# Gate and up products of a gathered expert in four strips of 128 columns, gate before up, and one turn of the hidden values

## The chip, the cores and the metric

One core of a Trainium2 chip runs one program. The time is the device time of one execution in microseconds (us); the program before was timed three times, and the median counts.

## The reference, cut to what matters

Two blocks on 256 tokens of 1024 values. The first holds two layers of four kinds of attention; the second a modulated layer with differential attention and pooling, and then a mixture of 32 experts in four groups. All is float32. The change lies in the experts:

```python
g_logits = (xt @ w_rg) + b_rg                 # 4 groups, the best one is taken
e_logits = ((xt @ w_re) + b_re).reshape(N, 4, 8)
top_p, top_i = lax.top_k(softmax(e_logits[tok, g_sel]), 2)
weights = g_p[:, None] * top_p / sum(top_p)
# for each expert e, over the tokens that chose it:
#   hidden = silu(x @ w_gate[e]) * (x @ w_up[e])      1024 -> 512
#   y     += weight * (hidden @ w_down[e])            512 -> 1024
x = x + g2 * y
```

Each expert has three matrices of 2 MiB: gate and up of 1024x512, down of 512x1024.

## The kernel before, in words

**Stages.** The attention layers and the projections come first, with weights loaded through a ring of six places of 2 MiB in SBUF (`ring`). The expert stage begins on TensorE after the router. Where no expert has more than 32 tokens (`crowd` is 0), it takes the gathered way, which this run takes; the dense way beside it is not executed.

**The gathered way.** Experts go in eight quads of four (`four_experts`, q the quad, s the expert in it). `gather` picks the tokens of a quad by a product with a selection matrix into `XG`, 32 columns for each expert. For an expert, TensorE does this:

- `gate_up` (lines 2400 to 2432): x times gate and x times up, in bank 1 of PSUM. The stationary side is the expert's 32 columns of `XG` for one of eight blocks of the contraction (k), so a product fills 32 of the array's 128 columns, and four strips stand side by side. Strips 0 and 1 are gate, 2 and 3 up; each holds half of the 512 hidden columns, 256 of them, namely columns 4f + 2(j mod 2) and the one behind it, two of every four. For each k all four strips follow each other. The last expert does its gate strips first and its up strips then. One increment of `g_gu` marks the end.
- ScalarE takes silu of gate on 64 partitions x 256 (line 943, `SIG`), VectorE multiplies by up (line 1737, `HID`).
- `turn_hidden` (lines 2434 to 2445) turns `HID` by two products with the identity, each reading every second column; ScalarE copies the result (line 950, `HG`).
- `down` (lines 2447 to 2463): four blocks of the hidden values, four strips of 256 output columns each; VectorE scales and stores them (line 1746), and `add_outputs` (line 2478) adds a quad's outputs to the sums.

Between these, quads interleave: after the first expert of a quad come `add_outputs` of the quad before and `turn_spread` (line 2470), after the second and third the two halves of the next `gather` (line 2398), and none of these after the fourth.

**The order of the loads.** All loads are issued by SP in an order written out by hand (lines 458 to 567). Experts 0 to 3 are loaded into the ring and into dead buffers before the stage. After the router's flag, `load_gathered` (line 529) waits for the place's last reader and issues one load: gate and up places are free with `g_gu`, down places with `g_down`. The order is gate, up and down of expert 4, then down of 3, gate and up of 5, gate of 6, down of 5, and from expert 6 on in turn; gate of every third expert of a quad lies in `probs` and waits for the one four before. A waiting load holds back all loads behind it. Down of expert 31 comes in two halves.

Of the kernel before, what the change touches and what calls it, by code (L numbers as in the profile page):

```python
# [8 lines left out]
P = 128  # L9
# [3 lines left out]
KD = D // P  # L13
# [6 lines left out]
NE = 32  # L20
FC = 4
CAP = 32
# [65 lines left out]
def build(nc, x, ab_w, ab_out_w, cd_w, cmp_w1, cmp_w2, uq_w, ukv_w, cd_out_w, ada_w, ada_b, in_w, pool_mt, pool_w,  # L88
          router_w, out_w, norm_rows, gate_w, up_w, down_w, consts, smalls, out):
    F32, BF16, U8 = mybir.dt.float32, mybir.dt.bfloat16, mybir.dt.uint8  # L90
    ALU, ACT, AX = mybir.AluOpType, mybir.ActivationFunctionType, mybir.AxisListType
    ctx = ExitStack()
    with ctx:
# [10 lines left out]
        def stages(suffix, adds):  # L104
            at = 0
            for tag, n in adds:
                stage_of[tag + suffix], before_stage[tag + suffix] = "all" + suffix, at
                at += n
# [5 lines left out]
        stages("_Ta", [(s[0], s[2]) for s in turned_stages])  # L114
        stages("_Tv", [(s[0], s[3]) for s in turned_stages])
        stages("_mm", [("abin", 12), ("about", 4), ("cdin", 12), ("cdout", 4), ("win", 8), ("wout", 4)])
        stages("_Pa", [("abin", 6), ("cdin", 6), ("win", 4)])
        stages("_Pv", [("abin", 6), ("cdin", 6), ("win", 4)])

        def upto(name, n):  # L120

            return sem(name), before_stage.get(name, 0) + n

        def sem(name):
            name = stage_of.get(name, name)
            if name not in made:
                made[name] = ctx.enter_context(nc.semaphore("s_" + name))
            return made[name]
# [38 lines left out]
        bank = [banks[:, i, :] for i in range(8)]  # L167
# [9 lines left out]
        def const(name, rows=P):  # L177
            a, n = CO[name]
            return C[0:rows, a:a + n]
# [5 lines left out]
        ident = const("ident")  # L185
# [38 lines left out]
        qt_flat = QT[:, :, :].rearrange("p a n -> p (a n)")  # L224
# [2 lines left out]
            return qt_flat[:, a:a + n].rearrange("p (k n) -> p k n", k=k)  # L227

        XG = part(0, 1024, KD)
        SIG = qt_flat[64:128, 2048:2304]  # L230
        HID = qt_flat[0:64, 2304:2560]
        HG = qt_flat[:, 2560:2688]
        ones = qt_flat[:, 2688:2816]
        YE = qt_flat[:, 2816:3840]
# [122 lines left out]
        def first_quad(q):  # L357
            return isinstance(q, int) and q == 0
# [8 lines left out]
        def hidden_psum(q):  # L367

            return bank[3] if last_quad(q) else bank[2][:, 256:512]
# [16 lines left out]
        def gathered_landed(eng, q, s, j):  # L386

            slot = eslot(3 * (s % 2) + j)
            if (s, j) == (2, 0):
                eng.wait_ge(*upto("ahead0", q * 16 + 16))  # L390
                return
            if not first_quad(q):
                if (s, j) == (0, 0):
                    eng.wait_ge(*upto(f"slot{slot}", q * 16 + (loads_of[slot] + 16)))
                    return
                skipped = 0 if s % 2 == 1 and j == 2 else 1
                eng.wait_ge(*upto(f"slot{slot}", q * 32 + (loads_of[slot] + 16 * (s // 2 + 1 - skipped))))
                return
            e = s
            ahead = {(2, 1): ("ahead1", 64), (2, 2): ("ahead2", 48), (3, 0): ("ahead3", 32),  # L400
                     (3, 1): ("ahead4", 16 * len(up3_homes))}
            if (e, j) in ahead:
                eng.wait_ge(*upto(*ahead[e, j]))
                return
            eng.wait_ge(*upto(f"slot{slot}", loads_of[slot] + 16 * (e // 2 + 1)))
# [15 lines left out]
        def _(sp):  # L421
# [7 lines left out]
            off, n, k, src = first_rows  # L429
            sp.dma_start(ring[0][:, off:off + n].rearrange("p (k n) -> p k n", k=k), src).then_inc(sem("ld_first"), 16)  # L430
            for i, (name, parts, _) in enumerate(chunks):
# [4 lines left out]
                if i >= SLOTS:  # L436
                    s, n = chunks[i - SLOTS][2]
# [90 lines left out]

            def load_gathered(j, e, freed_by):

                sp.wait_ge(*upto("g_down" if j % 3 == 2 else "g_gu", freed_by + 1))
                if e % 4 == 2 and j % 3 == 0:
                    load_third_gate(e)
                else:
                    load_expert(j, e)
# [69 lines left out]
        def _(act):  # L605
# [130 lines left out]
            act.activation(QT[:, 12, :], bank[5][:, 0:256], ACT.Copy).then_inc(sem("abi_Ta"), 1)  # L736
            query_squares(2, 1, scrA[:, 1536:2048])
            for t in range(NT):
                act.wait_ge(*upto("idx", t + 1))
                for odd in range(2):  # L740
                    act.activation(index_relu(t, odd), index_psum(t, odd), ACT.Relu).then_inc(sem("idx_r"), 1)
            act.wait_ge(*upto("ms", ROOT["abk1"]))
# [196 lines left out]
            def gathered_silu(e):  # L939
                act.wait_ge(*upto("g_gu", e + 1))  # L940
                if e > 0:
                    act.wait_ge(*upto("g_hid", e))
                act.activation(SIG, bank[1][0:64, 0:256], ACT.Silu).then_inc(sem("g_sig"), 1)  # L943

            def take_hidden(e):

# [28 lines left out]
        def _(v):  # L975
# [403 lines left out]
            pe = small("pe")  # L1379
# [6 lines left out]
            for half in range(2):  # L1386
                for g in range(2):
                    n = 16 - half
# [36 lines left out]
            a = SM["kvlat_col"][0]  # L1425
# [3 lines left out]
            a = SM["qlat_col"][0]  # L1429
# [111 lines left out]
            a = SM["lambdas"][0]  # L1541
# [191 lines left out]
            def hidden(e):  # L1733
                v.wait_ge(*upto("g_sig", e + 1))
                if e > 0:
                    v.wait_ge(*upto("g_ht", e))
                v.tensor_tensor(HID, SIG, bank[1][64:128, 0:256], ALU.mult).then_inc(sem("g_hid"), 1)  # L1737

            def outputs(e):

# [26 lines left out]
            with v.If(crowded == 0):  # L1767
                for e in range(NE):
                    q = e // 4
# [37 lines left out]
        def _(pe):  # L1807
# [240 lines left out]
            for t in range(NT):  # L2048
                K = P * (t + 1)
                for h in range(4):  # L2050
                    r = slice(64 * (h % 2), 64 * (h % 2) + 64)
                    ins = pe.matmul(bank[(2, 6)[t] + h % 2][:, (h // 2) * SEQ:(h // 2) * SEQ + K],
                                    QT[r, 10 + h // 2, t * P:(t + 1) * P], QT[r, 12, 0:K], start=True, stop=True)
                ins.then_inc(sem("idx"), 1)
            for t in range(NT):
                project_ab(3, t)
            pe.wait_ge(*upto("ab_k", 2))
# [82 lines left out]
            for g in range(2):  # L2140
                pe.matmul(bank[6][0:N_CMP, 64 + 64 * g:128 + 64 * g], hcT[:, 16 * g:16 * g + N_CMP], lat[:, 2560:2624],
                          start=True, stop=True)
# [259 lines left out]
            def gate_up(q, s):  # L2402

                e, last = expert_of(q, s)
                if s == 0:
                    pe.wait_ge(*upto("g_xc", q * 2 + 1))
                if not (first_quad(q) and s == 0):
                    pe.wait_ge(*upto("g_hid", e))
                wg, wu = gathered_weight(q, s, 0), gathered_weight(q, s, 1)

                def strip(k, j):
                    wk = (wg, wu)[j // 2](k).rearrange("p (f c) -> p f c", c=FC)
                    return pe.matmul(bank[1][CAP * j:CAP * j + CAP, 0:256], XG[:, k, CAP * s:CAP * s + CAP],  # L2413
                                     wk[:, :, 2 * (j % 2):2 * (j % 2) + 2], start=(k == 0), stop=(k == KD - 1))

                gathered_landed(pe, q, s, 0)
                if last:
                    for k in range(KD):
                        for j in range(2):
                            strip(k, j)  # L2420
                    gathered_landed(pe, q, s, 1)
                    for k in range(KD):
                        for j in range(2, 4):
                            ins = strip(k, j)
                else:
                    gathered_landed(pe, q, s, 1)
                    for k in range(KD):
                        if first_quad(q) and s == 0 and k == 4:
                            pe.wait_ge(*upto("g_xv", 1))
                        for j in range(4):  # L2430
                            ins = strip(k, j)
                ins.then_inc(sem("g_gu"), 1)

            def turn_hidden(q, s):

                e, last = expert_of(q, s)
                pe.wait_ge(*upto("g_hid", e + 1))
                if last_quad(q):
                    pe.wait_ge(*upto("g_hc", e))
                elif not (first_quad(q) and s == 0):  # L2440
                    pe.wait_ge(*upto("g_ye", e))
                for j in range(2):
                    ins = pe.matmul(hidden_psum(q)[:, 64 * j:64 * j + 64], HID[:, j:256:2], ident[0:64, 0:64],
                                    start=True, stop=True)
                ins.then_inc(sem("g_ht"), 1)

            def down(q, s):

                e, last = expert_of(q, s)
                if not last:  # L2450
                    gathered_landed(pe, q, s, 2)
                pe.wait_ge(*upto("g_hc", e + 1))
                if last_quad(q):
                    pe.wait_ge(*upto("g_ye", e))
                wd = gathered_weight(q, s, 2)
                for c in range(FC):
                    if last and c % 2 == 0:
                        pe.wait_ge(*upto(f"last_down{c // 2}", 16))
                    a = 64 * (c % 2) + CAP * (c // 2)
                    for n in range(4):  # L2460
                        ins = pe.matmul(bank[2][CAP * n:CAP * n + CAP, 0:256], HG[:, a:a + CAP],  # L2461
                                        wd(c)[:, 256 * n:256 * n + 256], start=(c == 0), stop=(c == FC - 1))
                ins.then_inc(sem("g_down"), 1)

# [183 lines left out]
```

## Time and profile before

| | us |
|---|---|
| median of 3 executions | 910.43 |
| lowest, highest | 907.78, 912.58 |
| the profiled execution | 911.11 |
| its span | 909.3 |
| TensorE busy in the span | 775.5 (85%) |
| VectorE, ScalarE busy | 373.5, 168.4 |
| bytes moved, mean rate | 284.38 MB, 313 GB/s |

The profile is of one execution. Its span is shorter than that execution's time by 1.8 us, which lie around it. Busy time of TensorE counts pipelined products, so a busy TensorE isn't at its peak. The granted clock of TensorE is given as a share of 2.4 GHz; it has two levels, 1.2 and 2.4 GHz, and a value between them is a mean over a stretch.

### The profile page before, as it was taken

Reading aid. Unit: us, or ns where it says so; the run is one execution under the profiler, and the core shown is the slowest. Engines: PE = TensorE matmul, PEld = TensorE weight load, DVE = VectorE, ACT = ScalarE, POOL = GpSimd, SP = SyncE. Lnnn points to the kernel's source line nnn. Section 1 sums busy time; section 2 is a strip of 40 time slices with the busy share of each in tenths; the row PEclk is TensorE's granted clock in tenths of the full one; section 3 lists DMA queues with packets and bytes.
Section 4 is the critical chain, followed back from the end, with each engine's and each line's share of the span. In section 5 each row is a group of like instructions: output and inputs, shape, how many; then the busy total and the mean of one; then the engine's idle time right before and its main releaser. Section 6 shows DMA issues by size and latency. Waiting matters only on the chain.

```text
span 909.3 us, 13058 instructions
## 1 busy us (share of the span) xinstructions
PE 775.5 (85%) x5393; PEld 465.6 (51%) x5393; DVE 373.5 (41%) x885; ACT 168.4 (19%) x473; POOL 40.5 (4%) x36
## 2 busy tenths in 40 slices
PE   7999899999998999999999987858766686677655
PEld 3544664456476644456578573535534444344332
DVE  2478668557854676766441212111111111121113
ACT  3222630223356301041120100000010100001001
POOL 1110000012400000001000000000000000000000
PEclk9999999999999999999999997889899889899888
DMA  9984506765002749987679999999999999999994
GB/s 343 394 291 155 186 1 241 269 231 186 1 1 82 277 130 352 392 338 321 232 269 396 406 425 430 430 430 427 426 427 429 430 428 429 427 428 429 427 428 162
DMA packets 54555, 284.38 MB, mean 313 GB/s; under 512 B 2800, under 2 KB 7280, under 8 KB 41968
## 3 DMA queue, kind: packets, MB, share of 16 engines
q1 hardware_dynamic: 54512, 283.81, 78.0%
q8 instruction: 27, 0.44, 0.2%
q14 instruction: 16, 0.13, 0.0%
HBM read 282.75 MB, written 1.05 MB: 312 GB/s over the span
## 4 chain that ended last, share of the span: by engine, by line
PE 55%; DMA 34%; DVE 5%; issue 2%; ACT 2%; POOL 1%; SPq 1%; DVEq 0%; POOLq 0%
DMA ring<-in_up_w 30%; PE banks L2002 15%; PE banks L1850 9%; PE banks L2413 8%; PE banks L2248 4%; DMA ring<-in_down_w 3%; PE banks L1954 3%; PE banks L2461 2%; PE banks L1882 2%; PE banks L2398 2%; DMA ring<-in_ada_w 1%; PE banks L1929 1%; POOL rs L590 1%; PE banks L1980 1%; PE banks L2492 1%
## 5 line engine op out<-in xcount | busy, mean ns | idle before, releaser
L2413 PE MATMUL banks<-ring,QT 128*32 128x256 f32 x1696 | 143.0, 445 | 56.7 <-DMA ring<-in_up_w 56.7
L2002 PE MATMUL banks<-ring,hT 128*128 128x512 f32 (+4 forms) x384 | 157.9, 566 | 2.4 <-DMA ring<-in_ab_w 2.1
L2413 PEld LDWEIGHTS banks<-ring,QT 128*32 128x32 f32 x1696 | 71.9, 123 | 105.7 <-DMA ring<-in_up_w 44.1
L2002 PEld LDWEIGHTS banks<-ring,hT 128*128 128x128 f32 x384 | 72.4, 193 | 75.5 <-issue 68.6
L1746 DVE TENSOR_TENSOR QT<-banks,MOD 32x256 f32<-32x256 f32 x128 | 53.8, 421 | 138.5 <-PE banks L2461 137.2
L1737 DVE TENSOR_TENSOR QT<-QT,banks 64x256 f32<-64x256 f32 x32 | 13.5, 423 | 191.4 <-ACT QT L943 191.4
L1850 PE MATMUL banks<-ring,hT 128*128 128x512 f32 x192 | 83.9, 594 | 1.9 <-ACT hT L628 1.8
L2461 PE MATMUL banks<-ring,QT 128*32 128x256 f32 x992 | 66.0, 408 | 14.6 <-ACT QT L950 12.4
L590 POOL TENSOR_TENSOR rs<-st,mhalf 128x1 f32<-128x1 f32 (+7 forms) x27 | 33.3, 1237 | 863.3 <-DVE st L1783 451.7
L943 ACT ACTIVATE QT<-banks 64x256 f32<-64x256 f32 x32 | 12.0, 375 | 294.4 <-PE banks L2413 294.4
L1185 DVE SCALAR_TENSOR_TENSOR extra<-ring,cs,extra 128x512 f32<-128x512 f32 x84 | 63.1, 752 | 2.9
L2413 PE MATMUL banks<-probs,QT 128*32 128x256 f32 x256 | 41.6, 492 | 25.1 <-DMA ring<-in_up_w 25.1
L1850 PEld LDWEIGHTS banks<-ring,hT 128*128 128x128 f32 x192 | 36.0, 190 | 46.9 <-issue 43.1
L2398 PEld LDWEIGHTS banks<-Y 128*128 128x128 f32 x224 | 54.4, 334 | 6.1 <-issue 6.1
L2398 PE MATMUL banks<-Y 128*128 128x128 f32 x224 | 57.1, 408 | 0.0
L2248 PE MATMUL banks<-ring,hT 128*128 128x512 f32 x128 | 56.5, 596 | 0.2 <-DVE MOD L1193 0.2
L2461 PEld LDWEIGHTS banks<-ring,QT 128*32 128x32 f32 x992 | 37.1, 114 | 31.2 <-issue 18.7
L664 ACT ACTIVATE probs<-banks,soft 128x256 f32<-128x256 f32 (+1 forms) x96 | 39.9, 432 | 32.9 <-DVE soft L1104 31.1
L2413 PEld LDWEIGHTS banks<-probs,QT 128*32 128x32 f32 x256 | 21.0, 136 | 42.6 <-issue 38.9
L2248 PEld LDWEIGHTS banks<-ring,hT 128*128 128x128 f32 x128 | 23.8, 190 | 30.9 <-issue 28.4
L2478 PE MATMUL banks<-QT,Y 128*128 128x512 f32 x64 | 31.2, 632 | 1.9 <-DVE QT L1746 1.9
L1094 DVE TENSOR_REDUCE soft<-banks 128x4 f32<-128x1024 f32 (+1 forms) x24 | 24.0, 1002 | 16.7 <-PE banks L1893 15.1
(361 smaller groups left out, 767.6 us busy)
## 6 DMA issues: line engine op xcount, KB each, us to landing
ring<-in_down_w SPq DMA_DIRECT2D x30, 2048.0 KB, 21.8
ring<-in_up_w SPq DMA_DIRECT2D x30, 2048.0 KB, 23.6
ring<-in_gate_w SPq DMA_DIRECT2D x23, 2048.0 KB, 20.4
ring<-in_ada_w SPq DMA_DIRECT2D x12, 2048.0 KB, 15.4
probs<-in_gate_w SPq DMA_DIRECT2D x8, 2048.0 KB, 29.2
ring<-in_ab_w SPq DMA_DIRECT2D x4, 2048.0 KB, 19.4
ring<-in_cd_w SPq DMA_DIRECT2D x4, 2048.0 KB, 13.5
ring<-in_in_w SPq DMA_DIRECT2D x4, 2048.0 KB, 14.5
```

Source lines behind the costliest of these rows:

```text
L590: pool.tensor_tensor(rs[0:r, a:a + k], st2[0:r, a:a + k], mhalf[0:r, a:a + k], ALU.pow)\
L664: act.activation(PB[:, u % 2, h * K:(h + 1) * K], score_of(u, h), ACT.Exp, bias=nmx[:, 4 * u + h:4 * u + h + 1], scale=scale, accum_out=sm ...
L1185: ins = v.scalar_tensor_tensor(out=acc, in0=w[:, k, :], scalar=by, in1=acc, op0=ALU.mult, op1=ALU.add)
L1746: ins = v.tensor_tensor(YE[CAP * s:CAP * s + CAP, 256 * c:256 * c + 256], bank[2][CAP * c:CAP * c + CAP, 0:256], MOD[CAP * s:CAP * s + CAP ...
L1850: ins = pe.matmul(bank[j % 4][:, 0:n], hT[:, k, t * P:(t + 1) * P], w[:, k, :], start=(k == 0), stop=(k == KD - 1))
L1954: ins = pe.matmul(value_bank(u)[:, P * h:P * h + v.shape[1]], PTB[:, u % 2, kb, h * P:(h + 1) * P], v, start=(kb == 0), stop=(kb == nb - 1))
L2002: ins = pe.matmul(bank[b][:, 0:n], hT[:, k, t * P:(t + 1) * P], w[:, k, :], start=(k == 0), stop=(k == KD - 1))
L2248: ins = pe.matmul(win_bank(c, t)[:, :], hT[:, k, t * P:(t + 1) * P], w[:, k, :], start=(k == 0), stop=(k == KD - 1))
L2398: ins = pe.matmul(bank[3 * half][:, P * k:P * k + P], Y[:, t, 4 * half + k:D:KD], SEL[:, t, :], start=(t == 0), stop=(t == NT - 1))
L2413: return pe.matmul(bank[1][CAP * j:CAP * j + CAP, 0:256], XG[:, k, CAP * s:CAP * s + CAP], wk[:, :, 2 * (j % 2):2 * (j % 2) + 2], start=(k ...
L2461: ins = pe.matmul(bank[2][CAP * n:CAP * n + CAP, 0:256], HG[:, a:a + CAP], wd(c)[:, 256 * n:256 * n + 256], start=(c == 0), stop=(c == FC ...
L2478: ins = pe.matmul(bank[4 + j][:, :], SWT[:, j // 2, :], YE[:, 512 * (j % 2):512 * (j % 2) + 512], start=False, stop=last)
```

## The change

The strips are cut anew. Gate and up are done one after the other, each in all four strips: strip n holds the hidden columns n, n + 4, n + 8 and so on, 128 of them, read as every fourth column of the weights. Gate goes to columns 0 to 127 of bank 1, up to 128 to 255. Gate only waits for its own load, and its end is marked by a semaphore of its own, for which the loads into gate places now wait. (A stage name is shared with two increments of an early index product, so that no further semaphore is taken.) Silu, product and `HID` lie on 128 partitions x 128 columns, and one transpose turns all of it. In `HG` block c now stands at 32c.

```diff
+        stages("_n", [("idx", 2), ("g_gate", NE)])
-        SIG = qt_flat[64:128, 2048:2304]
-        HID = qt_flat[0:64, 2304:2560]
+        SIG = qt_flat[:, 2048:2176]
+        HID = qt_flat[:, 2176:2304]
...
-                sp.wait_ge(*upto("g_down" if j % 3 == 2 else "g_gu", freed_by + 1))
+                sp.wait_ge(*upto(("g_gate_n", "g_gu", "g_down")[j % 3], freed_by + 1))
...
-                act.activation(SIG, bank[1][0:64, 0:256], ACT.Silu).then_inc(sem("g_sig"), 1)
+                act.activation(SIG, bank[1][:, 0:P], ACT.Silu).then_inc(sem("g_sig"), 1)
...
-                v.tensor_tensor(HID, SIG, bank[1][64:128, 0:256], ALU.mult).then_inc(sem("g_hid"), 1)
+                v.tensor_tensor(HID, SIG, bank[1][:, P:2 * P], ALU.mult).then_inc(sem("g_hid"), 1)
...
-                def strip(k, j):
-                    wk = (wg, wu)[j // 2](k).rearrange("p (f c) -> p f c", c=FC)
-                    return pe.matmul(bank[1][CAP * j:CAP * j + CAP, 0:256], XG[:, k, CAP * s:CAP * s + CAP],
-                                     wk[:, :, 2 * (j % 2):2 * (j % 2) + 2], start=(k == 0), stop=(k == KD - 1))
-
-                gathered_landed(pe, q, s, 0)
-                if last:
+                for w, j in ((wg, 0), (wu, 1)):
+                    gathered_landed(pe, q, s, j)
                     for k in range(KD):
-                        for j in range(2):
-                            strip(k, j)
-                    gathered_landed(pe, q, s, 1)
-                    for k in range(KD):
-                        for j in range(2, 4):
-                            ins = strip(k, j)
-                else:
-                    gathered_landed(pe, q, s, 1)
-                    for k in range(KD):
-                        if first_quad(q) and s == 0 and k == 4:
+                        if first_quad(q) and s == 0 and (j, k) == (0, 4):
                             pe.wait_ge(*upto("g_xv", 1))
-                        for j in range(4):
-                            ins = strip(k, j)
-                ins.then_inc(sem("g_gu"), 1)
+                        for n in range(4):
+                            ins = pe.matmul(bank[1][CAP * n:CAP * n + CAP, P * j:P * j + P], XG[:, k, CAP * s:CAP * s + CAP],
+                                            w(k)[:, n:512:FC], start=(k == 0), stop=(k == KD - 1))
+                    ins.then_inc(sem(("g_gate_n", "g_gu")[j]), 1)
...
-                for j in range(2):
-                    ins = pe.matmul(hidden_psum(q)[:, 64 * j:64 * j + 64], HID[:, j:256:2], ident[0:64, 0:64],
-                                    start=True, stop=True)
-                ins.then_inc(sem("g_ht"), 1)
+                pe.transpose(hidden_psum(q)[:, 0:P], HID, ident).then_inc(sem("g_ht"), 1)
...
-                    a = 64 * (c % 2) + CAP * (c // 2)
                     for n in range(4):
-                        ins = pe.matmul(bank[2][CAP * n:CAP * n + CAP, 0:256], HG[:, a:a + CAP],
+                        ins = pe.matmul(bank[2][CAP * n:CAP * n + CAP, 0:256], HG[:, CAP * c:CAP * c + CAP],
```

## Rows read from the trace of the kernel before

**Rows 1.** The page's 40 slices of 22.7 us: granted clock, transfers.

```profile
PEclk9999999999999999999999997889899889899888
DMA  9984506765002749987679999999999999999994
GB/s 343 394 291 155 186 1 241 269 231 186 1 1 82 277 130 352 392 338 321 232 269 396 406 425 430 430 430 427 426 427 429 430 428 429 427 428 429 427 428 162
```

**Rows 2.** The chain in order of time: start, us, engine or load.

```profile
494.94 3.50 PE banks L2461 x32
...
504.28 2.61 PE banks L2461 x32
...
527.05 1.93 PE banks L2461 x32
...
543.73 23.32 DMA ring<-in_up_w
...
865.55 24.50 DMA ring<-in_down_w
...
895.00 1.11 PE banks L2461 x16
```

**Rows 3.** Stretches: engines' busy us, then granted clock, DMA share, GB/s.

```profile
468.00:470.00 2.00, 2.00 (x40) 1.19 (x36) 1.69 (x7) 0.61 (x1) 0.00 (x0) 1.00 0.05 21
470.00:472.00 2.00, 1.80 (x30) 0.79 (x20) 0.11 (x1) 0.38 (x1) 0.00 (x0) 1.00 0.00 0
...
488.00:490.00 2.00, 2.00 (x35) 1.57 (x25) 0.00 (x0) 0.10 (x1) 0.00 (x0) 1.00 0.76 221
...
520.00:522.00 2.00, 2.00 (x37) 1.13 (x29) 0.12 (x1) 0.00 (x0) 0.00 (x0) 1.00 0.82 311
...
600.00:700.00 100.00, 69.30 (x724) 42.41 (x720) 17.28 (x41) 6.52 (x18) 0.00 (x0) 0.90 1.01 429
```

**Rows 4.** Timeline of SP's queue, 471 to 519 us: the loads' issues.

```profile
471.48 0.34 SPq L457 DMA_DIRECT2D ring<-in_gate_w  x1
...
475.50 11.08 SPq L457 DMA_DIRECT2D ring<-in_down_w  x2
486.62 0.43 SPq L457 DMA_DIRECT2D ring<-in_gate_w  x1
...
518.40 0.33 SPq L457 DMA_DIRECT2D ring<-in_down_w  x1
```

**Rows 5.** Timeline, expert 0 and its neighbours, 463 to 480 us.

```profile
463.18 0.29 DVE L1654 TENSOR_TENSOR Y<-C,PM 128x128 f32<-128x128 f32 x1
...
467.55 3.88 PE L2413 MATMUL banks<-ring,QT 128*32 128x256 f32 x64
...
471.36 0.44 PE L2470 MATMUL banks<-C,Y 128*128 128x128 f32 x2
...
471.49 0.38 ACT L943 ACTIVATE QT<-banks 64x256 f32<-64x256 f32 x1 [2.87 <-PE banks L2413]
...
471.89 0.42 DVE L1737 TENSOR_TENSOR QT<-QT,banks 64x256 f32<-64x256 f32 x1 [2.04 <-ACT QT L943]
...
472.37 0.68 PE L2443 MATMUL banks<-C,QT 64*128 64x64 f32 x4 [0.57 <-DVE QT L1737]
...
473.09 0.28 ACT L950 ACTIVATE QT<-banks 128x128 f32<-128x128 f32 x1 [1.23 <-PE banks L2443]
...
479.04 4.08 PE L2398 MATMUL banks<-Y 128*128 128x128 f32 x16
```

**Rows 6.** Lines apart and the chain: small products, weight loads at different spacings.

```profile
407.93 1.79 PE banks L1947 x16
...
L2125 PE MATMUL banks<-ring,probs 64*32 64x128 f32 x128 | 3.7, 271 | 0.0
...
L2398 PEld LDWEIGHTS banks<-Y x224: 312/336/338, 479.0 to 825.3; 128*128 128x128 f32 x112
...
L2443 PEld LDWEIGHTS banks<-C,QT x128: 189/193/193, 472.4 to 892.3; 64*128 64x128 f32 x128
```

More of the change, by code:

```diff
@@ L738, in _ @@
             for t in range(NT):
-                act.wait_ge(*upto("idx", t + 1))
+                act.wait_ge(*upto("idx_n", t + 1))
                 for odd in range(2):
@@ L2053, in _ @@
                                     QT[r, 10 + h // 2, t * P:(t + 1) * P], QT[r, 12, 0:K], start=True, stop=True)
-                ins.then_inc(sem("idx"), 1)
+                ins.then_inc(sem("idx_n"), 1)
             for t in range(NT):
```

## The prediction

> **What bounds the kernel now.** I read the slices of the page first, then the chain in order of time, the stretches of the expert stage, the loads' issues on SP, and expert 0 step by step. The slices [rows 1] show the transfers at 425 to 430 GB/s with the DMA engines at nine tenths from about 500 us on, and mostly less before it. The chain [rows 2] agrees: until 543.73 us it runs through TensorE, then each piece of some 25 us is a load of up weights, and the last ones are a load of down weights that lets TensorE go on at 895.00. So two things set the end: how soon the queue of loads becomes full for good, and 14.3 us of tail behind the last load (909.3 - 895.0). In between nothing counts unless it makes the queue run dry. A load is 2 MiB, 4.9 us at 428 GB/s; an expert needs three, 14.7 us. TensorE is busy 69% of 600 to 700 us, and partly at its lower clock (granted 0.90, a mean of 1.2 and 2.4 GHz) [rows 3].
>
> The queue is not full at first [rows 3]: it stands still for nearly all of 468 to 472 us, and 488 to 490 moves 221, 520 to 522 moves 311 GB/s. Against 428 those stretches lose 1.9 + 2.0 + 1.0 + 0.5 us; with the edges beside them some 7 us. The issues on SP [rows 4] say why: gate and up of expert 4 wait for expert 0's gate and up products (471.48), down of expert 3 for down of expert 1 (the second issue of the row that begins at 475.50, just before 486.62), down of expert 6 for down of expert 4 (518.40). After that the queue is never dry. The date that counts is therefore TensorE's end of expert 4, not that of any single load.
>
> **The change part by part.** *Gate place freed first.* Expert 0's products run 3.88 us from 467.55 [rows 5]. Gate is now half of the work and goes first, so its load can be issued at about 469.6 instead of 471.48, 1.9 us earlier. That alone doesn't reach the end: three loads follow, 14.7 us, and the next issue waits for down of expert 1, which this part doesn't move. From then on an earlier gate load only lengthens a queue that has enough. Worth 0 by itself at the end, 1.9 us at the first load. The order on SP is kept, so in all later rounds a freed gate place is taken only when the loads ahead of it are issued. The gate strips no longer wait for up's landing; TensorE then has half of the products done when up lands, but its waits there are covered by the transfers. No wait is added: the one for up moves behind the gate strips.
>
> *One turn instead of two products.* The turn of the hidden values takes 0.68 us (4 instructions on 64 partitions) [rows 5]. It becomes one transpose of 128x128. Two such transposes take 0.44 us [rows 5], and a product of 128 columns comes every 0.11 us (16 in 1.79, [rows 6]), so one is 0.33: 0.35 less per expert, on TensorE's chain whether or not gathers hide the rest. Five turns lie before 518.40: 1.75 us.
>
> *Silu and product on 128 partitions.* Now 64x256: 0.38 on ScalarE, 0.42 on VectorE. At 128x128 the neighbours are 0.28 (a copy out of PSUM) and 0.29 (a VectorE product) [rows 5]: 0.23 less. Behind experts 1 and 2 of each quad a gather covers it, behind expert 4 the output sums; it is exposed at experts 0 and 3: 0.46 us.
>
> *Strips of 128 columns.* 64 instructions of 256 columns become 128 of 128 columns, the same columns in all, four strips at once. Issue and weight loads: line 2125 runs 128 products of 128 columns on four tiles in 3.7 us [rows 6], against 3.88 now. So the doubled count costs nothing; a gain of 0.15 each would be 0.75 over five. I take 0. What that row doesn't show is the new reading: each column of a strip now stands 16 bytes from the next, where now two of every four are read together. No product in this trace reads its moving side so. From below: now, at two of four, 64 instructions take 3.88 and down's, contiguous, 32 take 1.93 [rows 2], the same pace, so that step cost nothing. From above: the gather's stationary side is read at every eighth column and 16 pairs take 4.08 us, where 16 contiguous pairs take 1.79 [rows 5, 6], 2.28 times; one weight load of 128 columns takes 336 ns there, and 193 in the turn, which reads every second column [rows 6]. At 2.28 times the products would take 8.8 us, 5.0 more. I take 0, because the moving side has so far kept its pace when half of each 16 bytes was skipped, and a strip has to fetch only one value in some 0.87 ns (1.79 us / 16 / 128); but the upper end stays as a rival of nearly the same weight.
>
> The Trainium skill speaks against the change here. SBUF — State Buffer, section "Door 1: The DMA port swizzle", says that SBUF is read in lines of 16 bytes, that at least two hits in a line are needed to hide its access, and that each new line is paid for. The old strips make two hits, the new ones one. The gather's row agrees with a price for it on the stationary side; for the moving side no row here tells. The same passage also calls a stride of four fp32 values free, which would give the sum below; by the rule of two hits it would be that of the first rival.
>
> *Last expert.* Its four half-filled products (gate strips, then up strips) fill all four strips now, some 3 us less of TensorE work. The second half of down still lands at about 895.0, so the tail keeps its 14.3 us: 0.
>
> **The sum.** 1.75 + 0.46 = 2.2 us earlier at the issue at 518.40. A check from the issue at 486.62: two turns and one exposed silu give 0.93 us, and about 1.2 us of idle transfer time after it can close up, 2.1. The profiled execution took 911.11 us (span 909.3), so it becomes 908.9; that execution stood 0.7 over the median of 910.43, and the median becomes 908.2.
>
> **The rivals.** *The strided strips read slower (slower).* Place: the five products before 518.40, where TensorE sets the dates. At the upper price 5 x 5.0 - 2.2 = 23 us later, 933; at 1.5 times, 5 x 1.9 - 2.2 = 7.5 later, 918. The loss stays, because from 522 us the queue of transfers has no slack to give back. At 2.28 times 5 us of 14.7 is 34% on top of the 69% busy, so TensorE would stand beside the transfers as the bound, at the full clock just holding. The middle is about 927. It decides from a factor of 1.11 on (0.44 us per expert eats the 2.2), and passes 0.5% at 1.35. For it: the gather's row. Against: the free step to two of four, and one value in 0.87 ns is slow. 0.39, of it 0.01 below 1.35.
>
> *Nothing arrives.* Because the changed dates fall on transfers that were in flight anyway: the idle between 486 and 522 is partly the ramp of a load after its issue and stays. Then -0.5 to +0.5, about 910.4. 0.13.
>
> *More arrives.* Down of expert 2 took 3.50 and of expert 3 2.61 us instead of 1.93 [rows 2], at the lower granted clock; that is 2.2 us of the chain before 518.40. If the denser products keep the clock up, they come back: 2.2 + 2.2, and 0.4 as half of what the strips may gain, give 905.6. 0.12, since what precedes these falls are steps that the change doesn't touch.
>
> **How the numbers follow.** A measurement of this kernel can tell about 0.5% (4.55 us) from no change; the three runs span 907.78 to 912.58. Forecast 0.36 and nothing arrives 0.13, with the 0.01 of hardly slower strips: 0.50 within 0.5%. Slower 0.38, faster 0.12. The likeliest case by itself is 906 to 911. The range must enter the rival of the slow strips: its cases lie from 915 to 933 and about 0.13 of them above 928; below 904.5 I leave 0.05. So 904.5 to 928.
>
> **What would show it.** Right: 128 instructions of one expert's products within 3.7 to 3.9 us; a turn of one instruction, 0.33; the first gate load issued near 469.6, down of expert 3 near 485.6 and down of expert 6 near 516.2; 428 GB/s from there to 892; the last down product released by its load near 892.8, and the same tail. Wrong: products of 5 us and more at the full clock, a new gap in the transfers ahead of the issue near 486 and again near 507 and 518, and TensorE in the chain beyond 543. If the strips are slow and the end isn't later, the reading of the full queue is wrong.

## The result and the profile after

The change makes the kernel slower. Its median is 925.54 us (4 runs, 921.49 to 928.94) against 909.64 us for the kernel before in the same session (4 runs, 907.78 to 912.58): 1.0173 times, 95% interval 1.0148 to 1.0198. That is 15.9 us. The profiled execution took 925.14 us, 14.0 more than the one of before; its span is 923.3 us.

The page of the changed kernel, its engines and the slices that answer to [rows 1]:

```profile
PE 845.9 (92%) x7345; PEld 537.0 (58%) x7345; DVE 368.6 (40%) x885; ACT 165.5 (18%) x473; POOL 40.5 (4%) x36
...
PEclk9999999999999999999999999999999999999998
...
GB/s 346 395 284 142 183 1 274 228 229 182 1 1 160 194 198 380 396 301 333 248 287 313 290 400 429 427 429 428 429 427 429 429 427 429 429 429 427 426 426 142
```

In these slices the granted clock stays at 9 up to the last but one, where before shows eights and a seven from the 28th on. The transfers reach 426 to 429 GB/s only from the 25th slice on, and the 21st to 23rd move 287, 313 and 290, where before moved 269, 396 and 406.

Timeline of the changed kernel, expert 0 (answers to [rows 5]; start, duration, instruction, and in brackets the wait ahead of it):

```profile
467.33 7.59 PE L2418 MATMUL banks<-ring,QT 128*32 128x128 f32 x128
...
475.01 0.28 ACT L944 ACTIVATE QT<-banks 128x128 f32<-128x128 f32 x1 [6.61 <-PE banks L2418]
475.32 0.29 DVE L1738 TENSOR_TENSOR QT<-QT,banks 128x128 f32<-128x128 f32 x1 [5.68 <-ACT QT L944]
475.66 0.33 PE L2430 MATMUL banks<-C,QT 128*128 128x128 f32 x1 [0.37 <-DVE QT L1738]
...
476.45 1.93 PE L2445 MATMUL banks<-ring,QT 128*32 128x256 f32 x32 [0.46 <-ACT QT L951]
```

The turn is 0.33, Silu 0.28 and the product on VectorE 0.29, to the hundredth what the prediction took. But the gate and up products take 7.59 us instead of 3.88, with the same columns in all.

Chain of the changed kernel in order of time (answers to [rows 2]):

```profile
492.31 7.37 PE banks L2418 x119
...
504.25 1.93 PE banks L2445 x32
506.19 7.36 PE banks L2418 x126
...
516.95 7.45 PE banks L2418 x120
...
663.31 7.55 PE banks L2418 x124
670.87 25.43 DMA ring<-in_up_w
...
908.33 1.59 PE banks L2445 x16
```

The chain runs through TensorE until 670.87 us, before until 543.73. The down products take 1.93 us at every expert; at experts 2 and 3 before took 3.50 and 2.61 at the lower granted clock. Those 2.2 us did come back.

SP's queue in the changed kernel (answers to [rows 4]; the second issue of the row with x2 is down of expert 3, the last two rows are down of experts 5 and 6):

```profile
471.24 0.34 SPq L458 DMA_DIRECT2D ring<-in_gate_w  x1
...
478.43 14.25 SPq L458 DMA_DIRECT2D ring<-in_down_w  x2
492.73 0.93 SPq L458 DMA_DIRECT2D ring<-in_gate_w  x1
...
517.00 0.33 SPq L458 DMA_DIRECT2D ring<-in_down_w  x1
...
530.79 0.33 SPq L458 DMA_DIRECT2D ring<-in_down_w  x1
```

The first gate load goes out at 471.24: half of products that are twice as long end where the whole ended before (471.48). Down of expert 3 goes out just before 492.73, 6.1 later than before, and down of expert 6 at 530.79, 12.4 later.

Two stretches, the changed kernel first, then the kernel before (columns as in [rows 3]):

```profile
480.00:520.00 40.00, 37.92 (x546) 30.12 (x542) 6.07 (x16) 2.64 (x8) 0.00 (x0) 1.00 0.76 306
520.00:600.00 80.00, 76.54 (x1038) 57.66 (x1034) 14.17 (x36) 4.31 (x14) 0.00 (x0) 1.00 0.98 407
600.00:700.00 100.00, 91.05 (x1274) 65.83 (x1264) 16.16 (x41) 5.84 (x18) 0.00 (x0) 0.98 1.01 429
```

```profile
480.00:520.00 40.00, 37.22 (x410) 27.58 (x413) 9.16 (x22) 3.21 (x9) 0.00 (x0) 0.91 0.99 403
520.00:600.00 80.00, 64.75 (x710) 43.64 (x702) 14.03 (x34) 4.89 (x14) 0.00 (x0) 0.89 1.00 425
```

Here the time went. The transfers lost (403 - 306) x 40 / 428 = 9.1 us in the first stretch and (425 - 407) x 80 / 428 = 3.4 us in the second, together 12.4 before rounding. With the tail, 15.0 instead of 14.3 us, that is 13.1 of the 14.0 us between the two spans; the other 0.9 us was not traced. From 600 us on both kernels move 427 to 429 GB/s, and nothing is given back.

### The profile page after: what moved, and what is told of

Read it like the earlier page. It is cut to its first block, busy times and chain, and to the rows that moved or that the text cites. A ratio compares the mean times of both kernels' runs of the same rounds, so it can differ in the third digit from the quotient of the medians.

```text
span 923.3 us, 16949 instructions
## 1 busy us (share of the span) xinstructions
PE 845.9 (92%) x7345; PEld 537.0 (58%) x7345; DVE 368.6 (40%) x885; ACT 165.5 (18%) x473; POOL 40.5 (4%) x36
## 4 chain that ended last, share of the span: by engine, by line
PE 68%; DMA 23%; DVE 4%; ACT 2%; issue 1%; POOL 1%; SPq 0%; DVEq 0%; POOLq 0%
DMA ring<-in_up_w 19%; PE banks L2418 16%; PE banks L2003 15%; PE banks L1851 9%; PE banks L2249 6%; PE banks L2445 4%; PE banks L2399 3%; DMA ring<-in_down_w 3%; PE banks L1955 2%; PE banks L1883 2%; PE banks L2462 2%; PE banks L1981 1%; PE banks L1930 1%; PE banks L1829 1%; POOL rs L591 1%
## 5 line engine op out<-in xcount | busy, mean ns | idle before, releaser
L2418 PE MATMUL banks<-ring,QT 128*32 128x128 f32 x3392 | 204.0, 409 | 22.9 <-DMA ring<-in_up_w 12.7
L2418 PEld LDWEIGHTS banks<-ring,QT 128*32 128x32 f32 x3392 | 139.9, 127 | 81.6 <-DMA ring<-in_up_w 21.3
L1738 DVE TENSOR_TENSOR QT<-QT,banks 128x128 f32<-128x128 f32 x32 | 9.2, 288 | 222.7 <-ACT QT L944 222.7
L2445 PE MATMUL banks<-ring,QT 128*32 128x256 f32 x992 | 60.7, 383 | 17.4 <-ACT QT L951 12.4
L944 ACT ACTIVATE QT<-banks 128x128 f32<-128x128 f32 x32 | 8.9, 278 | 321.9 <-PE banks L2418 321.9
L2445 PEld LDWEIGHTS banks<-ring,QT 128*32 128x32 f32 x992 | 34.6, 109 | 35.3 <-issue 17.6
L2418 PE MATMUL banks<-probs,QT 128*32 128x128 f32 x512 | 31.2, 408 | 2.6 <-DMA probs<-in_gate_w 2.6
L1955 PEld LDWEIGHTS banks<-Y,probs 128*128 128x128 f32 x192 | 23.3, 192 | 9.4 <-ACT probs L677 5.8
## 6 DMA issues: line engine op xcount, KB each, us to landing
ring<-in_in_w SPq DMA_DIRECT2D x4, 2048.0 KB, 14.3
```

The costliest lines, as they stand in the source:

```text
L1955: ins = pe.matmul(value_bank(u)[:, P * h:P * h + v.shape[1]], PTB[:, u % 2, kb, h * P:(h + 1) * P], v, start=(kb == 0), stop=(kb == nb - 1))
L2418: ins = pe.matmul(bank[1][CAP * n:CAP * n + CAP, P * j:P * j + P], XG[:, k, CAP * s:CAP * s + CAP], w(k)[:, n:512:FC], start=(k == 0), sto ...
```

## The experiments

Four theories are named in the expectations. SPACING: a TensorE product runs at half its pace when each moving value stands in another 16 bytes. COUNT: the products are slow because there are twice as many. FETCH: beside that, the added instructions of TensorE cost some us, because TensorE has to fetch its program while the weight loads fill the DMA engines. ORDER: what is left over comes from gate first and its earlier load. Each kernel was measured against the kernel before on the same chip, whose median lay between 908.32 and 909.02 us.

### 1. The same products, with near columns

```diff
-    w(k)[:, n:512:FC]
+    w(k)[:, P * n:P * n + P]
```

The down load and its rows are left as they are, so the hidden values meet other rows of the down weights than in the reference.

> The changed kernel, but strip n reads 128 columns side by side (128n to 128n+127) in place of every fourth; down is left as it is, so hidden values meet other rows of down (the output is that of permuted weights). Theory SPACING (a product streams at half pace when each of its moving columns lies in another 16 bytes): the 128 instructions of gate and up fall from 7.4 to about 3.7 us, the 5 expert products before the issue of down of expert 6 give back 18 us, and the time is 906 to 909 us. Theory COUNT (an instruction on a 128x32 tile costs about 57 ns, whatever its width: 64 in 3.62 before, 128 in 7.38 after): still 7.4 us, and 922 to 928 us.

Measured: 912.27 us (10 runs, 909.09 to 916.43), 1.0049 times before (1.0034 to 1.0065). Chain of this kernel:

```profile
466.59 3.67 PE banks L2418 x128
...
473.66 3.49 PE banks L2418 x128
...
494.66 1.52 PE banks L2418 x55
496.18 2.36 issue
498.54 2.25 PE banks L2418 x73
...
517.26 2.09 issue
...
540.45 1.57 issue
```

128 instructions take 3.49 to 3.67 us again: COUNT is not what halved the pace. With this one slice the loss against the kernel before falls from 15.9 to 4.0 us, so it gives back some 12. The rows marked "issue" are new: TensorE stands still in the middle of the products, at 496.18 between 55 and 73 of the 128 instructions, and waits for nothing that the profile shows. The changed kernel has no such row inside its slow products. In this execution (909.09 us, the fastest of the ten) down of expert 6 goes out at 514.67, 3.7 us earlier than before, yet the median of the ten is 4 us above the median before.

### 2. Near columns with the down load to match

```diff
-    "e (p c) n -> p (e c) n"   # down_w
+    "e (c p) n -> p (e c) n"
```

> As c2, and down is loaded so that partition p holds rows p, 128+p, 256+p and 384+p (four pieces of 4 KB in place of one of 16 KB for each partition): this computes the same as the kernel before. If the pieces of 4 KB move as fast as those of 16 KB, c1 equals c2 within 1 us under either theory. If they cost, the 65 MB of down slow the full queue: 5% on them would be 7 us more.

Measured: 917.81 us (4 runs, 916.43 to 920.78), 1.0099 times before (1.007 to 1.0128), 5.5 us over experiment 1. Each partition's down values now come as four pieces of 4 KB instead of one of 16 KB. Slices of its page:

```profile
GB/s 340 394 310 131 184 1 277 229 231 183 1 1 144 214 180 379 393 318 322 226 317 393 366 419 423 420 425 418 423 419 425 418 428 418 427 417 425 418 420 147
```

417 to 425 GB/s in nearly all of the last slices, instead of 427 to 429: a mean of 421 against 428 over some 366 us is 6 us. So the simple way to near columns that computes the same gives back on the loads 5.5 of the some 12 us that it wins.

### 3. The kernel before, with its 256 columns spread out

```diff
+    at = 1024 * (k // 2) + j
+    wk = whole[:, at:1024 * (k // 2) + 1024:FC]
```

64 instructions as before, but each reads every fourth value of a double span (experts 2 and 3 keep their old reading). The products read other weights than in the reference.

> The kernel before with its 64 instructions of 256 columns, but each reads every fourth value of a span of 1024 instead of two of every four of 512, except in experts 2 and 3 of the first quad (wrong weights meet the tokens, the same number of columns and instructions). Theory SPACING: 64 instructions take about 7.3 us in place of 3.7 and the kernel ends 10 to 17 us later than before (three slowed products before 518 us instead of five, then TensorE nearly full). Theory COUNT: 3.7 us and the time of before.

Measured: 929.42 us, one execution, span 927.6. Its chain, expert 0 and, unchanged, expert 2:

```profile
467.28 7.41 PE banks L2418 x64
...
493.19 3.67 PE banks L2418 x62
```

The line number is another, the count of 64 is that of before. No added instruction, no moved load, no new turn, and 7.4 us against 3.67. SPACING alone doubles the products and makes a loss at least as large as the change's; COUNT falls. The 21 us over before miss the 10 to 17 that were expected. Here the last expert keeps its half-filled strips, gate first and up then, and they take 11.17 us at the end of the chain, where before took 6.6; with one execution the rest of the miss stays open.

### 4. Spacings side by side

At the end of TensorE's work in the changed kernel 24 products of each kind were added, whose results nothing reads (192, 96 or 48 instructions: a product in fp32 is two, and four strips are four products). No loads run there.

> The changed kernel with products added at TensorE's end that nothing reads: first 24 of 512 columns, then groups of 24 products (48 instructions) of 128 columns with the moving side read at steps 1, 2, 4, 8 of a value on the full 128x128 array; then 24 rounds of four strips (192 instructions) at steps 1, 2, two of four, 3, 4, 8, 16; then 24 rounds of two strips and of one strip at steps 1 and 4. Theory SPACING as a property of one stream: full-array products take 0.11 us per instruction at steps 1 and 2 and 0.21 at 4 and 8; a round of four strips (8 instructions) 0.21 at 1, 2 and two of four, 0.43 at 4, 8 and 16, step 3 between them. SPACING as a width shared by four streams: full-array and one-strip groups are equal at steps 1 and 4, two strips little slower, four strips twice as slow. Theory COUNT: every group of four strips 57 ns per instruction, at any step.

Timeline of the added products. In order: full array with step 1, 2, 4; four strips with step 1, 2, two of four, 3, 4, 8; two strips with step 4; one strip with step 1, 4. Ahead of them ran the 24 products of 512 columns. The left-out rows among the others are full array with step 8 (11.38 us), four strips with step 16 (11.50) and two strips with step 1 (5.43).

```profile
937.78 5.52 PE L2520 MATMUL banks<-ring,QT 128*128 128x128 f32 x48
943.13 5.61 PE L2522 MATMUL banks<-ring,QT 128*128 128x128 f32 x48
948.58 11.04 PE L2524 MATMUL banks<-ring,QT 128*128 128x128 f32 x48
...
970.75 5.45 PE L2529 MATMUL banks<-ring,QT 128*32 128x128 f32 x192
976.01 5.63 PE L2532 MATMUL banks<-ring,QT 128*32 128x128 f32 x192
981.46 5.62 PE L2535 MATMUL banks<-ring,QT 128*32 128x128 f32 x192
986.90 8.53 PE L2538 MATMUL banks<-ring,QT 128*32 128x128 f32 x192
995.24 11.22 PE L2541 MATMUL banks<-ring,QT 128*32 128x128 f32 x192
1006.26 11.42 PE L2544 MATMUL banks<-ring,QT 128*32 128x128 f32 x192
...
1033.99 11.15 PE L2553 MATMUL banks<-ring,QT 128*32 128x128 f32 x96
1044.96 5.42 PE L2556 MATMUL banks<-ring,QT 128*32 128x128 f32 x48
1050.22 11.04 PE L2559 MATMUL banks<-ring,QT 128*32 128x128 f32 x48
```

Steps of 4 and 8 bytes and two of every four values cost the same within some 3%; 12 bytes cost 1.55 times; 16 bytes 2.0 to 2.1 times, and 32 and 64 bytes 2.1. An estimate that is worked out from these rows fits them: let each 16 bytes that are touched cost as much as two values at least. A step of 12 bytes then touches three of them for four values, 6 / 4 = 1.5 times, a step of 16 bytes four, 2.0 times, and all steps and pairs with two or more values in each 16 bytes are free. One strip, two or four make no difference, and the full array pays the same. So the price is paid by each stream for itself, and the slow read of one is not hidden behind the other three. Four strips with step 1 also show 192 instructions in 5.45 us with no halt, where no load runs beside them.

The Trainium skill's page SBUF — State Buffer, section "Door 1: The DMA port swizzle", asks for two hits in a line of 16 bytes; by that rule the trace agrees, steps 1 and 2 and two of four being free and step 4 double. The same passage of the Trainium skill calls a stride of four fp32 values free; the rows of step 4 contradict it, 11.22 us against 5.45 on four strips.

### 5. The kernel before, each product of 256 columns cut in two

```diff
-    for k in range(KD):
-        for j in range(4):
-            ins = strip(k, j)
+    for half in range(2):
+        for k in range(KD):
+            for j in range(4):
+                ins = strip(k, j, half)
```

> The kernel before, with each of its products of 256 columns cut into two of 128 (two of every four columns, as before; all of the first halves, then all of the second): the same result, 128 instructions for an expert, nothing else moved. Theory FETCH (what is left of the loss with near columns, 912.3 against 908.3 us, comes from the number of TensorE instructions: their code is fetched through the same DMA engines, and TensorE stalls inside the products, 0.6 + 2.4 + 2.1 us ahead of 520 us in that profile): stalls of 1 to 3 us inside the products of the first experts appear here too, and the time is 2 to 5 us over before. Theory ORDER (the loss comes from gate going first and from what that does to the queue of loads): products 3.5 us as with near columns, no stall of more than 0.5 us, time within 1.5 us of before.

Measured: 912.68 us (10 runs, 911.39 to 914.33), 1.0041 times before (1.0024 to 1.0058): 4.0 us for the count alone, with two of four read as before. Its waits and chain:

```profile
PE banks L2413 <- issue: 5.9, 4, 2.0
```

```profile
520.64 1.98 issue
...
884.93 9.35 PE banks L2413 x119
...
897.31 0.94 issue
```

The halts, 1.0 to 2.0 us each, are like those of experiment 1, and they are there without gate first and without near columns. The row at 884.93 cannot be read as a price of the count: the last expert's products take 9.35 us where before took 6.58, but the granted clock stood at 0.50 from 884 to 890 us here and at 1.00 there. Down of expert 6 goes out at 518.15, no later than before (518.40), so in this execution the early halts do not move that date, and where the 4 us arise was not measured. That it is the fetch of TensorE's program that halts it is argued, not shown. For it: the page counts 27 packets on the instruction queue before and no halt inside the products, 29 and two halts in experiment 8, 33 and four halts here and in experiment 1; and the added products of experiment 4 show no halt where no load runs. The changed kernel has 33 packets too and no halt, with products that take twice as long.

### 6 and 7. The gate's place freed with up's, as before

```diff
-    ("g_gate_n", "g_gu", "g_down")[j % 3]
+    ("g_gu", "g_gu", "g_down")[j % 3]
```

Experiment 6 has this edit on the kernel of experiment 1 (which computes with other rows of down, as there), experiment 7 on the changed kernel.

> Near columns in four strips as c2, but loads into gate places wait for the end of up again (one wait undone, on SP alone). FETCH: within 1.5 us of c2 (912.3), since the freed place is worth nothing at the end. ORDER: 2 to 4 us faster than c2, near before.

> The changed kernel (every fourth column) with the loads into gate places waiting for the end of up. With products of 7.4 us the gate place comes free 3.7 us earlier in the changed kernel than here. If only TensorE's dates of the down products count, the time is that of the changed kernel within 1 us; if the early gate covers part of the loss, it is 2 to 4 us slower.

Measured: 914.36 us (8 runs, 911.81 to 916.81) on near columns, 1.0054 times before (1.0034 to 1.0074), against 1.0049; and 925.47 us (4 runs) on the changed kernel, 1.0184 (1.0156 to 1.0213), against 1.0173. In experiment 7 the first gate load goes out at 474.66 instead of 471.24, and down of expert 6 at 530.28 instead of 530.79. So freeing the gate's place earlier is worth nothing at the end, within some 2 us. Undoing it does not remove the 4 us either: experiment 6 lies 5.7 us over before, 1.7 more than experiment 1, a little outside the 1.5 that was expected under FETCH. Together with experiment 5, where gate does not go first at all, ORDER falls.

### 8. The new form for experts 0 to 3 only, with near columns

Experts 0 to 3 in the changed form with near columns and down in 4 KB pieces, all others as before: few added instructions and few cut loads, at the place where dates count.

```diff
+    early = "g_gate_n" if freed_by < 4 else "g_gu"
```

and the same distinction at each line of the change.

> A kernel that computes the reference: experts 0 to 3 in the new form with near columns (their down loaded in pieces of 4 KB, before the stage), experts 4 to 31 as before. Each of the four saves about 0.35 us in the turn and 0.35 in the products, two of them 0.23 in silu and product: down of expert 4 ends about 3 us earlier, the queue of loads is full 3 us earlier, 905 to 906 us. FETCH takes back 1 to 3 us of it, since the code of the first quad grows by 256 pairs of instructions: 906 to 909.

Measured: 910.74 us (12 runs, 908.54 to 912.98), 1.0023 times before (1.0008 to 1.0038): a miss, 1.7 us above the highest value expected. Its chain:

```profile
487.34 1.44 issue
...
497.66 2.91 issue
```

Down of expert 6 goes out at 518.34, as before (518.40). The two halts, 4.35 us, eat what the turns and the clock give. Why the median lies 2 us over before with that date unchanged is not shown.

### 9 to 12. Near values for the gather's stationary side

If 16 bytes cost a factor of two wherever TensorE reads, the gather, which every quad of both kernels does at a step of eight values, must gain too, and with it the dates. Experiments 9 and 10 write the rows so that the gather reads 128 neighbours, on the kernel before and on the changed one; they also permute the rows that an earlier layer reads, so these two work on other values than the reference. Experiments 11 and 12 do it for the expert layer's rows alone:

```diff
+    y = Y[:, t, 0:D].rearrange("p (k n) -> p n k", k=KD)[:, 64 * c:64 * c + 64, :]
...
-    Y[:, t, 4 * half + k:D:KD], SEL[:, t, :]
+    Y[:, t, P * (4 * half + k):P * (4 * half + k) + P], SEL[:, t, :]
```

> The kernel before, with the normed rows written so that the 128 columns of each block stand side by side (VectorE writes and reads at a step of 8 there instead), and the gathers and the last transposes read them so: the same result, the same TensorE instructions. SPACING on the stationary side too: 16 instructions of a gather take 1.8 us instead of 4.08; the stage of experts starts 3 to 4 us earlier, two gathers before the down product of expert 4 give 4.5 us more, and the load that waits for it is issued about 8 us earlier. Since the queue of loads cannot be full sooner than its first load is issued, 4 us earlier, and some 3 us of its idle time can close up: 902 to 904 us. If VectorE pays for the step of 8 in its two operations, 1 to 2 us of that is lost. If a gather is bound by something else, 4.08 us stay and the time is that of before.

> The changed kernel (every fourth column) with the same near gather. If the end is set by TensorE's dates in the first experts and by the full queue of loads after them, the gathers give back here at least what they give to the kernel before: 3.9 us at the start, 2.2 for each of the gathers up to about 545 us (four of them), some 10 us less than the changed kernel, 914 to 918 us. If TensorE bound the loads to the end, the gain would be larger than 20 us (14 gathers of 2.2).

> As n1_before_near_gather, but only the rows that the experts and the router read are laid out anew; n1 moved those of the layer before too, so that it worked on other values (903.9 us). The same result as the kernel before. TensorE's instructions, their sizes and the loads are those of n1, so 902 to 905 us, 4 to 6 less than before; gathers of 1.8 us, the load that waits for down of expert 4 issued 7 to 8 us earlier than in the kernel before.

> As an_after_near_gather with the rows of the experts and the router alone laid out anew: the changed kernel's result, 916 to 920 us (an had 917.6). Its distance to n2 is what every fourth column costs when the gathers are cheap: the same 12 to 17 us as between the changed kernel and the one before.

Measured on the kernel before: 903.94 us (6 runs), 0.9949 times (0.9931 to 0.9967), and for the expert layer alone 905.03 us (8 runs, 904.59 to 907.9), 0.9961 times (0.9947 to 0.9975). On the changed kernel: 917.55 us, 1.0103 (1.007 to 1.0136), and 918.33 us, 1.0103 (1.0087 to 1.012). Experiment 11 computes what the reference does and is faster than both kernels of this case. Its rows, the gather by line, then the timeline with the second of VectorE's two writers and half a gather of the first quad, SP's issues, and a stretch:

```profile
L2403 PE MATMUL banks<-Y 128*128 128x128 f32 x224 | 28.7, 281 | 0.0
```

```profile
445.91 2.08 DVE L1634 SCALAR_TENSOR_TENSOR Y<-Y,rs,MOD 128x1024 f32<-128x1024 f32 x1 [0.67 <-POOL rs L590]
...
459.30 2.03 PE L2497 MATMUL banks<-Y 128*128 128x128 f32 x16
```

```profile
468.43 0.34 SPq L457 DMA_DIRECT2D ring<-in_gate_w  x1
...
507.99 0.33 SPq L457 DMA_DIRECT2D ring<-in_down_w  x1
```

```profile
480.00:520.00 40.00, 37.23 (x528) 26.25 (x519) 11.37 (x27) 3.59 (x10) 0.00 (x0) 1.00 1.01 427
```

Sixteen gather instructions take 2.0 us (28.7 / 14) instead of 4.08, so the stationary side pays a factor of two at this step as well. The first gate load goes out 3.1 us and down of expert 6 10.4 us earlier, and 480 to 520 us move 427 GB/s, a full queue. Only 4 us reach the end. A queue that is nearly full gains little from earlier dates: before left (428 - 403) x 40 / 428 = 2.3 us of transfers unused from 480 to 520 and 0.6 from 520 to 600, with the 3.1 at the start 6.0 in all. It is the same reading as of the loss, from the other side. In the profiled execution the last half of down begins 5.0 us earlier, at 889.97 instead of 895.00, and runs at a granted clock of 0.52 (890 to 892 us), and the span ends 4.3 earlier. VectorE pays a little, 1.06 and 2.08 us where the same writes took 0.69 and 1.28. On the changed kernel the distance to experiment 11 stays 13.3 us: an earlier start does not cure slow products, which hold the queue at 324 GB/s over the same 480 to 520 us in experiment 12.

## Why the prediction was wrong

It had the mechanism that came true among its rivals, and chose another as likeliest: the forecast was 908.2 us, and the first rival, the strided strips, came true with 925.54, inside the range and next to that rival's middle of 927.

*Strips of 128 columns* is the step that failed. It took 0 for the reading at 16 bytes, "because the moving side has so far kept its pace when half of each 16 bytes was skipped, and a strip has to fetch only one value in some 0.87 ns". Both halves of that argument are refuted. Two of four is free and one of four is double (experiment 4): the first row said nothing about the second. And one value in 0.87 ns is too fast for this reading: a single strip that reads far values takes 11.04 us where near ones take 5.42. The other bound came from the gather, whose stationary values also lie in separate 16 bytes; it was set at 2.28 times, and near rows make it 2.0. It was the nearer cousin, and the products came out at 7.4 us, 1.9 times, not 8.8. With 7.4 the rival's own sum gives 5 x (7.4 - 3.88) - 2.2 = 15.4 us, and 15.9 were measured. That this is so close is partly luck, since the parts behind it differ, as told below: the date moved by 12.4, and the rest was added elsewhere.

*The count costs nothing*, of the same step, was mis-sized for near reads. The row of line 2125 [rows 6] rightly gave some 3.7 us for 128 instructions (experiment 1: 3.49 to 3.67), but it is one stretch of 3.7 us, with the DMA engines at 0.85 and 262 GB/s, and could not show a halt that comes now and then. The doubled count costs 4.0 us (experiment 5), with halts of 1.0 to 2.0 us. In the changed kernel itself it costs nothing that shows: at 7.4 us for 128 instructions none of its products halts.

*One turn*: 0.33 us, as taken, but under-counted. Behind a gather or the output sums the chain held 0.62 us of turn before and holds 0.12 now, so three of the five save 0.50 and two 0.35: 2.2 us, not 1.75. *Silu and product*: 0.28 and 0.29 us, as taken.

*Gate place freed first*: 0 at the end (experiment 7). The 1.9 us at the first load did not come either, only 0.24, since half of 7.59 us is no shorter than 3.88.

*The date of down of expert 6 decides*: right. In the two chains the five products took 7.58 + 7.41 + 7.37 + 7.36 + 7.45 = 37.2 us instead of 19.5, so +17.6; the turns -2.2, Silu and product -0.5; the five down products -2.4, of which 2.2 at experts 2 and 3 are the mechanism of the rival "more arrives", which did happen and was covered; the start 0.2 earlier. That makes 12.4, and the issue moved by 12.4. Then the full queue keeps it: 427 to 429 GB/s from 600 us on.

*Last expert*: the 3 us less did not come. Its gate strips take 3.87 us and its up strips about as much, together more than the 6.58 of before, but off the path. *The tail*: 15.0 instead of 14.3 us; 0.5 of it is the last half of down, 1.59 us instead of 1.11, at a granted clock that fell from 0.88 to 0.50 within 908 to 910 us. *TensorE as the bound*: it is busy 91% of 600 to 700 us and the transfers stay full; at a factor of 2 it holds beside them, as the rival had it.

*The signs that it listed*: products over 5 us at the full clock, new gaps in the transfers near 486 and 507 to 518, the chain through TensorE beyond 543. All three came.

## What to carry to other kernels

Look at the byte step of every operand of a TensorE product, moving and stationary, and keep at least two fp32 values of each 16 bytes together; here a step of 16 bytes or more doubled the time whatever the number of strips, and a layout written near by the producer cost VectorE 0.4 to 0.8 us for each write. Where an unseen read has one bound from a cousin with pairs side by side that is free and another from a cousin whose values stand as far apart that is slow, take the one with the spacing. Ask at each change whether TensorE sets the dates of the loads at that place: a loss there stays for good once the queue is full, a gain there is capped by it, and count added instructions as a cost of their own: they took 4 us here.

## What the runs showed of the hardware that was not expected

- A step of 12 bytes costs 1.55 times, between free and double.
- Four strips that each read slowly take no longer together than one alone (11.22, 11.15 and 11.04 us for four, two and one): they run side by side, but none hides the slow read of another.
- Halts of TensorE inside a run of products, with no wait in the profile, where its products are short and many and the loads are full: 6.6 us in four halts (experiment 1), 5.9 in four (experiment 5), none among the added products of experiment 4. The cause is not shown.
- The time at the lower clock is not lost where it is covered, but it is on the dates: the granted clock was 1.00 in 480 to 520 us instead of 0.91, and two down products got 2.2 us back. That a busier TensorE keeps the clock up does not follow: it was busy for 37.9 of these 40 us in the changed kernel and 37.2 before, while experiment 1 had 1.00 with 32.4 and experiment 3 had 0.91 with 37.7.
- Down weights in pieces of 4 KB instead of 16 KB cost 5.5 us of 915 (experiment 2 against 1).
